# A third set of weight buffers in the expert loop, slots in threes, and the next slot's gate products ahead of the down products

## The reference, cut to what matters

```python
def hier_moe(h, P, l):
    ...
    grp = jnp.argmax(grp_logits, axis=-1)
    ...
    top_val, top_idx = lax.top_k(in_grp, EXPERT_TOP)
    w_top = jax.nn.softmax(top_val, axis=-1) * p_grp
    eid = grp[:, None] * GROUP_EXPERTS + top_idx
    ...
    for e in range(N_EXPERTS):
        act = jax.nn.silu(hf @ P['moe_w_gate'][l, e]) * (hf @ P['moe_w_up'][l, e])
        out = out + combine[:, e:e + 1] * (act @ P['moe_w_down'][l, e])
```

## Time and profile before

| | |
|---|---|
| median of three runs | 2293.39 us (2292.13 to 2295.51) |
| profiled execution, its own time | 2304.49 us |
| its span, first to last instruction | 2302.7 us |
| PE busy, share of the span | 83% |
| mean granted clock of PE over the span | 0.908 |
| wu loads issued, both layers | 32, of 2048 KB |
| bytes moved | 400.62 MB, 174 GB/s over the span |

### The profile page before, as it was taken

How to read it: one execution, slowest core, us unless ns; L and a number is a source line. 1 busy time by engine, 2 the same in 40 slices (tenths; PEclk the granted TensorE clock), 3 DMA queues, 4 the chain that set the end, 5 groups by cost and what they waited for, 6 DMA issues and landing times.

```text
span 2302.7 us, 53637 instructions
## 1 busy us (share of the span) xinstructions
PE 1907.1 (83%) x23824; PEld 1527.2 (66%) x23824; DVE 677.7 (29%) x1831; ACT 506.4 (22%) x1111; POOL 81.1 (4%) x135
## 2 busy tenths in 40 slices
PE   5598996988788777599996499999999975999863
PEld 3376764776667656488886345987666755888763
DVE  3300024465655522200111402012777231101014
ACT  1110112333333202100010401002777130000002
POOL 1000004100000000100000000000000001000000
PEclk8699997898989978799998799997999987999996
DMA  5578736600000024599996914233000255999952
GB/s 192 186 278 272 274 125 198 206 13 12 12 12 12 13 65 177 224 376 376 377 380 228 270 77 98 72 95 92 2 2 2 72 223 206 377 364 364 366 189 80
DMA packets 175621, 400.62 MB, mean 174 GB/s; under 512 B 50967, under 2 KB 112883, under 8 KB 167187
## 3 DMA queue, kind: packets, MB, share of 16 engines
q1 hardware_dynamic: 157234, 345.55, 43.3%
q0 software_dynamic: 11040, 39.85, 5.0%
q10 hardware_dynamic: 7168, 12.59, 1.5%
HBM read 346.47 MB, written 55.68 MB: 175 GB/s over the span
## 4 chain that ended last, share of the span: by engine, by line
PE 68%; DVE 8%; DMA 8%; issue 6%; ACT 5%; DVEq 2%; SPq 2%; POOL 1%; ACTq 0%; POOLq 0%
PE bank L1493 8%; PE bank L406 7%; PE bank L1308 5%; PE bank L1488 5%; DMA wu<-in_moe_w_up_dram 4%; PE bank L2068 4%; PE bank L1506 3%; PE bank L1512 3%; PE bank L2119 3%; PE bank L369 2%; PE bank L609 2%; PE bank L2162 2%; PE bank L2214 2%; DMA adaw<-in_ada_w_dram 2%; PE bank L2251 2%
## 5 line engine op out<-in xcount | busy, mean ns | idle before, releaser
L1506 PE MATMUL bank<-wd,actT 128*32 128x384 f32 x1536 | 171.6, 488 | 26.6 <-ACT actT L1609 26.6
L1488 PE MATMUL bank<-wg,xsT 128*32 128x384 f32 x1536 | 173.4, 492 | 7.9 <-DMA wu<-in_moe_w_up_dram 6.6
L1493 PE MATMUL bank<-wg,xsT 128*32 128x128 f32 x1536 | 175.5, 275 | 0.0
L1493 PE MATMUL bank<-wu,xsT 128*32 128x128 f32 x1536 | 172.9, 273 | 0.0
L1512 PE MATMUL bank<-wd,actT 128*32 128x256 f32 (+1 forms) x1024 | 172.4, 327 | 0.0
L1488 PE MATMUL bank<-wu,xsT 128*32 128x384 f32 x1536 | 170.8, 486 | 0.0
L1493 PEld LDWEIGHTS bank<-wg,xsT 128*32 128x32 f32 x1536 | 168.7, 111 | 1.6
L1493 PEld LDWEIGHTS bank<-wu,xsT 128*32 128x32 f32 x1536 | 167.7, 110 | 0.0
L406 PE MATMUL bank<-xm,wp 128*128 128x272 f32 x512 | 122.9, 399 | 17.8 <-DVE xm L561 17.8
L1761 DVE TENSOR_TENSOR act<-bank,act 128x384 f32<-128x384 f32 x32 | 17.8, 558 | 403.6 <-PE bank L1493 403.6
L1512 PEld LDWEIGHTS bank<-wd,actT 128*32 128x32 f32 x1024 | 109.6, 110 | 23.3
(11 more groups left out here) (520 smaller groups left out, 3822.9 us busy)
## 6 DMA issues: line engine op xcount, KB each, us to landing
wg<-in_moe_w_gate_dram SPq DMA_DIRECT2D x32, 2048.0 KB, 16.0
wu<-in_moe_w_up_dram SPq DMA_DIRECT2D x32, 2048.0 KB, 20.9
wd<-in_moe_w_down_dram SPq DMA_DIRECT2D x32, 2048.0 KB, 20.7
adaw<-in_ada_w_dram SPq DMA_DIRECT2D x48, 1024.0 KB, 7.9
wp<-in_rwkv_w_rkv_dram SPq DMA_DIRECT2D x24, 512.0 KB, 3.7
xs<-x_slots SPq DMA_DIRECT2D x32, 384.0 KB, 18.2
x_slots<-zeros POOLq DMA_DIRECT2D x21, 512.0 KB, 14.2
y_slots<-zeros POOLq DMA_DIRECT2D x21, 512.0 KB, 14.1
```

The source lines that it names most:

```text
L1488: mm = pe.matmul(ps[32 * j:32 * j + 32, 0:GW], B.xsT[:, k, 32 * j:32 * j + 32], w[:, k, 0:GW], start=k == 0, stop=k == KT - 1)
L1493: mm = pe.matmul(ps[96:128, q * 128:(q + 1) * 128], B.xsT[:, kk, 32 * q:32 * q + 32], w[:, kk, GW:FF], start=kk == 0, stop=kk == KT - 1)
L1506: mm = pe.matmul(bank[4 + b][32 * j:32 * j + 32, 0:384], act_piece(k, j), w[:, k, b * 384:(b + 1) * 384], start=k == 0, stop=k == 3)
```

## The change

Three things are done together. The slots are counted as one and then threes: slot 0, then rounds v of three slots (buffers 1, 2, 0), so that slot s uses buffer s % 3. The straight code holds slot 0 and round 0, the loop does one round (three slots) per turn, and the last round is straight code again. For 16 slots this makes 1 + 3 slots, three turns of the loop, and 3 slots. The number of slots that DRAM has room for stays 28.

The third set of buffers lies in space that something else uses earlier: wg[2] on the buffers wo of the output projection, wu[2] on fT, wd[2] on ga (the token rows, and later the gathered ones), xs[2] on hs. Their first loads wait for the last reader of that space: wg[2] for out_mm, wu[2] for the token transposes (h_tr), wd[2] and xs[2] for the scatter. ys gets a third buffer of its own, and cmp5 shares the scratch scan.

On PE the order for slot s becomes: up, both halves of the turn of slot s + 1, transposes of act, gate of slot s + 1, down of slot s. The gate products of slot 0 come ahead of everything. On ACT the silu of slot s + 1 stands behind the copy of actT of slot s and ahead of the copy to ys.

```diff
-SLOTS = E_N + OVER + (E_N + OVER) % 2
+TRIPS = 5 + -(-OVER // 3)
+SLOTS = 1 + 3 * TRIPS
...
-    B.cmp5 = sb(st, "cmp5", [128, 16, T // C])
+    B.cmp5 = B.scan[:, 0:T // C].rearrange("p j e -> p (j e)").rearrange("p (e j) -> p e j", e=16)
...
-    B.ga = [sb(st, f"ga{i}", [128, D]) for i in range(4)]
-    B.xs = [sb(st, f"xs{i}", [C, D]) for i in range(2)]
-    B.hs = sb(st, "hs", [NS, D])
-    B.ys = [sb(st, f"ys{i}", [128, YW]) for i in range(2)]
+    B.gall = sb(st, "gall", [128, 4, D])
+    B.ga = [B.gall[:, i, :] for i in range(4)]
+    B.hx = sb(st, "hx", [128, D])
+    B.xs = [sb(st, f"xs{i}", [C, D]) for i in range(2)] + [B.hx[0:C]]
+    B.hs = B.hx[0:NS]
+    B.ys = [sb(st, f"ys{i}", [128, YW]) for i in range(3)]
...
-    B.wg = [sb(st, f"wg{i}", [128, KT, FF]) for i in range(2)]
-    B.wu = [sb(st, f"wu{i}", [128, KT, FF]) for i in range(2)]
-    B.wd = [sb(st, f"wd{i}", [128, 4, D]) for i in range(2)]
-    B.wo = [sb(st, f"wo{i}", [128, KT, 128]) for i in range(4)]
+    B.wg = [sb(st, f"wg{i}", [128, KT, FF])[:] for i in range(2)]
+    B.wu = [sb(st, f"wu{i}", [128, KT, FF])[:] for i in range(2)]
+    B.wd = [sb(st, f"wd{i}", [128, 4, D])[:] for i in range(2)]
+    w3 = sb(st, "w3", [128, KT * FF])
+    B.wo = [w3[:, 1024 * i:1024 * i + 1024].rearrange("p (k n) -> p k n", k=KT) for i in range(4)]
+    B.wg.append(w3[:].rearrange("p (k n) -> p k n", k=KT))
+    B.wu.append(B.fT[:].rearrange("p k t -> p (k t)")[:, 0:KT * FF].rearrange("p (k n) -> p k n", k=KT))
+    B.wd.append(B.gall[:])
...
+def prior_uses(regs, l, v, j):
+
+    if v is None:
+        return before(regs, l) + l
+    return v + before(regs, l) + (l + 1 if j == 0 else 0)
+
+
+def uses(regs, l, v, j):
+
+    return prior_uses(regs, l, v, j) + 1
+
+
+def local_slot(v, j):
+
+    return 0 if v is None else 3 * v + (j or 3)
+
+
+def slot_count(regs, l, v, j):
+
+    return 3 * before(regs, l) + l + local_slot(v, j)
...
     for i in range(2):
         load_gate_up(i, i)
         load_down(i, i)
+    sp.wait_ge(S("out_mm"), 16 * (l + 1))
+    load_gate(2, 2)
+    sp.wait_ge(S("h_tr"), 10 * (l + 1))
+    load_up(2, 2)
     sp.wait_ge(S("route_step"), 5 * l + 5)
-    regs.append(sp.value_load(B.pairs[l][0:1, 0:1], min_val=E_N // 2 - 1, max_val=SLOTS // 2 - 1))
+    regs.append(sp.value_load(B.pairs[l][0:1, 0:1], min_val=4, max_val=TRIPS - 1))
     sp.wait_ge(S("scattered"), 160 * (l + 1))
-    for i in range(2):
+    for i in range(3):
         load_tokens(i, i)
-    with sp.Fori(1, regs[l] + 1) as t:
-        for i in range(2):
-            slot = 2 * t + i
-            last = (t - 1 + before(regs, l)) * 2 + i
-            e = sp.value_load(B.slot_e[0:1, bass.ds(slot, 1)], min_val=0, max_val=E_N - 1)
-            sp.wait_ge(S("x_tr"), last * 2 + 2)
-            load_tokens(i, slot)
-            sp.wait_ge(S("up_mm"), last * 4 + 4)
-            load_gate_up(i, e)
-            sp.wait_ge(S("downa_mm"), last * 4 + 4)
-            sp.wait_ge(S("downb_mm"), last * 4 + 4)
-            load_down(i, e)
-
-    for i in range(2):
-        sp.wait_ge(S(f"ys_stored{i}"), (regs[l] + 1 + before(regs, l)) * 32)
+    load_down(2, 2)
+
+    def following(v, j):
+        n = slot_count(regs, l, v, j)
+        slot = local_slot(v, j) + 3
+        e = sp.value_load(B.slot_e[0:1, bass.ds(slot, 1)], min_val=0, max_val=E_N - 1)
+        sp.wait_ge(S("x_tr"), n * 2 + 2)
+        load_tokens(j, slot)
+        sp.wait_ge(S("up_mm"), n * 4 + 4)
+        load_gate_up(j, e)
+        sp.wait_ge(S("downa_mm"), n * 4 + 4)
+        sp.wait_ge(S("downb_mm"), n * 4 + 4)
+        load_down(j, e)
+
+    following(None, 0)
+    with sp.Fori(0, regs[l]) as v:
+        for j in (1, 2, 0):
+            following(v, j)
+
+    for j in range(3):
+        sp.wait_ge(S(f"ys_stored{j}"), uses(regs, l, regs[l], j) * 32)
     sp.nop().then_inc(S("ys_complete"), 1)
...
-    def turn(i, n, h):
+    def turn(j, n, h):
...
-    def slot(i, t, first, last):
-        n = t + before(regs, l)
-        s = n * 2 + i
-        pe.wait_ge(S("xt_ev"), s * 2 + 2)
-        pe.wait_ge(S(f"wgu_loaded{i}"), n * 32 + 32)
-        gate_or_up(B.wg[i], bank[0], "gate_mm")
-        gate_or_up(B.wu[i], bank[1], "up_mm")
+    def slot(v, j, last):
+        n = prior_uses(regs, l, v, j)
+        s = slot_count(regs, l, v, j)
+        v2, j2 = (v, (j + 1) % 3) if j else (0 if v is None else v + 1, 1)
+        gate_or_up(B.wu[j], bank[1], "up_mm")
         if not last:
-            turn(1 - i, n + i, 0)
+            for h in range(2):
+                turn(j2, uses(regs, l, v2, j2), h)
         pe.wait_ge(S("act_ready"), s + 1)
         for c in range(3):
             mm = pe.transpose(bank[2 + c // 2][:, c % 2 * 128:c % 2 * 128 + 128], B.act[:, c, :], B.ident[:])
         mm.then_inc(S("at_mm"), 1)
         if not last:
-            turn(1 - i, n + i, 1)
+            pe.wait_ge(S("xt_ev"), s * 2 + 4)
+            pe.wait_ge(S("silu_done"), s + 1)
+            pe.wait_ge(S(f"wgu_loaded{j2}"), uses(regs, l, v2, j2) * 32)
+            gate_or_up(B.wg[j2], bank[0], "gate_mm")
         pe.wait_ge(S("at_ev"), s * 2 + 2)
-        pe.wait_ge(S(f"wd_loaded{i}"), n * 16 + 16)
-        if not (first and i == 0):
+        pe.wait_ge(S(f"wd_loaded{j}"), n * 16 + 16)
+        if l or v is not None:
             pe.wait_ge(S("ys_ev"), s * 2)
-        down(B.wd[i])
+        down(B.wd[j])
 
     for h in range(2):
-        turn(0, before(regs, l), h)
+        turn(0, uses(regs, l, None, 0), h)
+    pe.wait_ge(S("xt_ev"), slot_count(regs, l, None, 0) * 2 + 2)
+    pe.wait_ge(S("wgu_loaded0"), uses(regs, l, None, 0) * 32)
+    gate_or_up(B.wg[0], bank[0], "gate_mm")
     slots(pe, regs, l, slot)
...
-    def slot(i, t, first, last):
-        n = t + before(regs, l)
-        s = n * 2 + i
+    def silu(s):
         act.wait_ge(S("gate_mm"), s * 4 + 4)
         act.activation(B.act[:].rearrange("p c t -> p (c t)"), bank[0][:, 0:GW], ACT.Silu).then_inc(S("silu_done"), 1)
+
+    def slot(v, j, last):
+        n = prior_uses(regs, l, v, j)
+        s = slot_count(regs, l, v, j)
+        at = local_slot(v, j)
         if not last:
             keep_turned(s + 1)
         act.wait_ge(S("at_mm"), s + 1)
         act.activation(B.actT[:, 0:2].rearrange("p c t -> p (c t)"), bank[2][:, 0:256], ACT.Copy).then_inc(S("at_ev"), 1)
+        if not last:
+            silu(s + 1)
         act.wait_ge(S("downb_mm"), s * 4 + 4)
-        if not first:
-            act.wait_ge(S(f"ys_stored{i}"), n * 32)
-        act.activation(B.ys[i][:, 384:YW], bank[5][:, 0:384], ACT.Copy).then_inc(S("ys_ev"), 1)
+        if not isinstance(n, int) or n > 0:
+            act.wait_ge(S(f"ys_stored{j}"), n * 32)
+        act.activation(B.ys[j][:, 384:YW], bank[5][:, 0:384], ACT.Copy).then_inc(S("ys_ev"), 1)
         act.wait_ge(S("ys_ev"), s * 2 + 2)
-        act.dma_start(B.y_slots.rearrange("(s c) n -> c s n", c=C)[:, bass.ds(t * 2 + i, 1), 0:YW].rearrange("c s n -> c (s n)"), B.ys[i][0:C, :])\
-            .then_inc(S(f"ys_stored{i}"), 16)
-        act.dma_start(B.y_slots.rearrange("(s q p) n -> p s q n", q=QT, p=32)[:, bass.ds(t * 2 + i, 1), :, YW:D].rearrange("p s q n -> p (s q) n"),
-                      B.ys[i][C:128, :].rearrange("p (q n) -> p q n", q=QT)).then_inc(S(f"ys_stored{i}"), 16)
-
-    keep_turned(before(regs, l) * 2)
+        act.dma_start(B.y_slots.rearrange("(s c) n -> c s n", c=C)[:, bass.ds(at, 1), 0:YW].rearrange("c s n -> c (s n)"), B.ys[j][0:C, :])\
+            .then_inc(S(f"ys_stored{j}"), 16)
+        act.dma_start(B.y_slots.rearrange("(s q p) n -> p s q n", q=QT, p=32)[:, bass.ds(at, 1), :, YW:D].rearrange("p s q n -> p (s q) n"),
+                      B.ys[j][C:128, :].rearrange("p (q n) -> p q n", q=QT)).then_inc(S(f"ys_stored{j}"), 16)
+
+    keep_turned(slot_count(regs, l, None, 0))
+    silu(slot_count(regs, l, None, 0))
...
-    slot(0, 0, True, False)
-    slot(1, 0, True, False)
-    with eng.Fori(1, regs[l]) as t:
-        for i in range(2):
-            slot(i, t, False, False)
-    slot(0, regs[l], False, False)
-    slot(1, regs[l], False, True)
+    slot(None, 0, False)
+    for j in (1, 2, 0):
+        slot(0, j, False)
+    with eng.Fori(1, regs[l]) as v:
+        for j in (1, 2, 0):
+            slot(v, j, False)
+    for j in (1, 2, 0):
+        slot(regs[l], j, j == 0)
...
-    dve.scalar_tensor_tensor(out=N["t"][:], in0=B.idx[:], scalar=2.0, in1=over.to_broadcast([128, 16]), op0=ALU.mult, op1=ALU.is_lt)
+    dve.scalar_tensor_tensor(out=N["t"][:], in0=B.idx[:], scalar=3.0, in1=over.to_broadcast([128, 16]), op0=ALU.mult, op1=ALU.is_lt)
...
-    ts(B.pairs_f[:], B.pairs_f[:], float(E_N // 2 - 1), None, ALU.add)
+    ts(B.pairs_f[:], B.pairs_f[:], 4.0, None, ALU.add)
...
-    def slot(i, t, first, last):
-        n = t + before(regs, l)
-        s = n * 2 + i
+    def slot(v, j, last):
+        n = prior_uses(regs, l, v, j)
+        s = slot_count(regs, l, v, j)
         dve.wait_ge(S("silu_done"), s + 1)
```

(30 more changed lines are left out.)

6 lines of the change are left out of this document (3 added, 3 removed).

## The result

The changed kernel takes 2313.16 us (median of 4 runs, 2310.28 to 2320.09) against 2294.45 us for the kernel before on the same chip (4 runs, 2292.13 to 2299.99): ratio 1.0081 [1.0056, 1.0107], 0.8% slower. Forecast was 2270, with 0.05 for slower.

A forecast was written before the change was run, and what follows sets the result against it. It took PE's pace to bound layer 0, and PE's then DMA's to bound layer 1. Layer 0: -14.0 + 3.3 + 0.6 = -10.1; layer 1: -14.0 - 7.6 + 8.1 = -13.5; together -23.6 from 2293.39, so 2270 us, range 2259 to 2283.

The forecast's parts named there:

- PE has to fetch its loop again: Rival: each of two backward jumps per layer waits 4 us for instructions; layer 0 loses 8 us; 2278 us; chance 0.26.
- 8.1 us wait: In layer 1, PE wants slot 15's wu at 2184.1 and gets it at 2192.2.
- 7 or 8 blocks: Instruction blocks of 256 that a loop body of three slots, 1699 PE instructions, was said to touch.
- The price: Cost of a fetch at each backward jump: bounds 2.4 and 8.6 us, taken as 4 us.
- My upper bound of 8.6 us: Highest cost of one loop fetch, from the median y_slots store beside a full q1; would leave no gain, 2296 us.
- The cover: Layer 1's loop fetches were to cost nothing, as its 8.1 us wait for wu takes them up.
- The 7.6 us of old waits in layer 1: Second expert stage's extra length in the earlier profile, put down to waits for wu; subtracted as -7.6 us.
- The join: Between gate/up and down of successive slots: 2.46 us shrinks to 1.53, at 15 joins, 14.0 us saved per layer.
- The early loads: Third set's loads ahead of the stage delay layer 0's scatter by 0 to 3.4 us, taken as 3.3; layer 1 nothing.
- DMA close behind PE: Slot 15's wu lands late for PE: waits of 0.6 us in layer 0 and 8.1 us in layer 1.

The follow-up runs named there:

- once3: The changed kernel with rounds 0 to 2 written as straight code, so no engine jumps backward: 2278.99 us, ratio 0.9921 to the kernel before.
- short3: The changed kernel in its own loop, with 21 of 24 narrow up products per slot left out (body of 1469 PE instructions): 2276.18 us, one run.
- mid3: The changed kernel in its own loop, with 12 of 24 narrow up products per slot left out (body of 1577 PE instructions): 2277.21 us, one run.
- fit3: The changed kernel with 87 and 74 dummy transposes ahead of the loop (layers 0 and 1), moving its body in the program: 2275.45 us, ratio 0.9919.
- off3: The changed kernel with 160 and 100 dummy transposes ahead of the loop, its body lying in 8 blocks: 2317.02 us, ratio 1.0102.
- align3: The changed kernel with 100 and 75 dummy transposes ahead of the loop, its body lying in 7 blocks: 2302.41 us, ratio 1.0026.
- before_again: The kernel before, unchanged, executed again for a second profile: 2290.84 us.
- late_up: Straight code of the changed kernel (once3), with the third wu's early load issued behind the scatter and the tokens of slots 0 to 2: 2278.05 us, ratio 0.9937.
- new2: The new order of PE and ACT alone, with two sets of buffers in straight code, against once2: 2318.74 us, ratio 1.0087 to the kernel before.
- once2: The kernel before with pairs 0 to 5 written as straight code, so its loop does one turn: 2305.92 us, ratio 1.0041.

## Why the prediction was wrong

**The step that failed** is that the sum puts the fetching of the loop at nothing. It stands only as the rival "PE has to fetch its loop again", with a chance of 0.26, a price of 4 us per jump, and the sentence that "layer 1 loses nothing, as its 8.1 us wait takes it up". In the runs the fetch came at every jump of the changed kernel; without it the stages are 288.0 and 286.2 us long (once3), with it 302.0 and 311.8.

*The chance.* The profile of before could not speak about three slots. Counting the instructions and their place in the compiled program, with the rule that the prediction quotes, could have. The Trainium skill, "Runtime: NRT & Kernel Launch", section "Instruction fetch mechanics", names 2048 instructions for PE in blocks of 256. The runs agree with that size: bodies over 5, 6 and 7 blocks were kept (the kernel before, short3, mid3, fit3), over 8 not (off3), nor over 7 when the jump lies 42 or 37 instructions ahead of the block's end (align3). They do not agree with the same section's warning that a jump finds only a window of two pages; here the measurement decides, and by the earlier trace rows it did so before the change. The prediction's "7 or 8 blocks" left open on which side the loop would fall, and the runs show that this decides.

*The price.* Compare the changed kernel with once3, whose waits for wu (3.6 us in layer 0 and 1.8 + 0.6 in layer 1) lie in the same stages. Without them once3's stages are 284.4 and 283.8 us. The changed kernel's are 17.6 and 28.0 us longer. Of this 12.7 and 19.2 are the pauses themselves, and 4.9 and 8.8 are left. PE's work at clock 0.50 behind the jumps, 11.2 and 11.7 us per layer, loses half its length, 5.6 and 5.9 us: enough for the rest of layer 0, and two thirds of that of layer 1, where some 3 us stay open. So a jump costs 8.8 us in layer 0, where there is one pause per jump, and 14.0 in layer 1, where there are two. I took 4. My upper bound of 8.6 us, from a y_slots store beside a full q1, was close to layer 0's; I chose the other end, "as a packet is only 16 KB". All these jumps came while the DMA share was about 1; that the full queues make the pause long is likely, but no run has a fetch beside quiet queues. The half clock after the pause was in no term.

*The cover.* The wait of 8.1 us that was to hide layer 1's pauses was itself made from the pace of one execution. In once3 2.4 us of it showed, in fit3 0.3. The pauses did take up what there was, as the changed kernel has no wait for wu left, but that is 3.6 and 2.4 us: 14.0 and 25.6 us of loss remain against once3 as it ran. And a load is only issued when PE releases its buffer, so during the pauses of layer 1 the loads fell back too (321 GB/s, share 0.84).

**The 7.6 us of old waits in layer 1** were no property of the kernel. before_again has none of them. Both terms built on them, -7.6 and +8.1, nearly cancelled, which is why the forecast of a kept loop hardly suffered. That was luck.

**The join** was right: 1.54 us against 1.53, pitch 17.36 against 17.34.

**The early loads**: the scatter moved by 1.7 us in the changed kernel and by 2.4 in once3 (6.15 against 3.74), where I took 3.3 out of 0 to 3.4; late_up gave 2.46 of it back. A size, in the stated bounds. One slip goes with it: the scatter ends before the stage begins, so these 3.3 us can't lengthen the stage. By its own terms the prediction's stage of layer 0 is 283.5 us (296.9 - 14.0 + 0.6) and not "about 287".

**DMA close behind PE** was right in kind and not in size. In once3 PE waited 3.6 and 2.4 us for wu, where the forecast had 0.6 and 8.1. Slot 15's wu landed 263.4 us (1211.6) and 261.7 us (2173.4) after the first transposes; the forecast had 259.0 and 266.5. The pace was 19.6 us per slot in layer 0 and 19.4 in layer 1, not 19.07 and 19.74. new2 shows what the order meets without the third set.

**Without the fetch the sum comes near, in part by luck.** Forecast: stages of 283.5 (see above) and 291.0 us, 23.6 us saved, a ratio of 2269.8 / 2293.4 = 0.9897. Measured: 288.0 and 286.2 in once3, too long by 4.5 and too short by 4.8, which cancel; 17 us saved by the medians of once3 and 20 by those of fit3. Against before_again (296.8 and 296.4) once3's stages save 8.8 and 10.2 us, and the scatter takes back 2.4: 16.6 us. Ratios are 0.9921 and 0.9919, with intervals that hold the forecast, but the same code as once3 on another chip gave 0.9940 [0.9918, 0.9962], and late_up 0.9937 [0.9902, 0.9972], which do not. So the sign is shown, and 12 to 20 us of the 23.6.

**Left open.** once2 is 0.4% slower than the kernel before, which keeps its loop. Its wu loads land every 19.6 us in layer 0 instead of 19.1, and q8 has more to bring, but a rate of 10 packets of 16 KB in 80 us (1100 to 1180) is too little to be the cause by volume, and in the changed order fit3 and once3 can't be told apart (0.9919 and 0.9921). What the fetching of straight code costs is not settled. Where exactly between 42 and 46 the line runs was not tried, nor whether other engines have such a line. Why some jumps have two pauses and others one is not known either.

## What to carry to other kernels

Before a loop body is lengthened, count the instructions that PE runs in a turn, in blocks of the size that q8 brings, with one more fetched ahead and some 50 behind the jump. If it no longer fits, each turn pays for a fetch through full DMA queues and for a restart at a lower clock; write the turns out, or move the body to where it fits. A wait that is to cover a loss should be seen in more than one execution first. And two parts that look weak or harmful alone (4 to 8 us gained and 13 lost here) may be worth 27 together, when one makes an engine faster and the other feeds it.
